# Expert pairs taken in another order, two of them before the routing is known, in a one-core network kernel

## The reference, cut to what matters

```python
def compress_blocks(x, pos_emb, w1, w2):          # once for keys, once for values, in each layer
    ...
    blk = blk.transpose(0, 1, 3, 2, 4).reshape(b_, n_cmp, NSA_GROUPS, CMP_LEN * NSA_DH)
    return jax.nn.silu(blk @ w1) @ w2             # w1: 32*64 x 64

def moe_ffn(h, w_router, w1, w3, w2):
    logits = (h @ w_router).astype(jnp.float32)
    top_val, top_idx = lax.top_k(logits, TOP_K)
    top_w = jax.nn.softmax(top_val, -1)
    combine = jnp.sum(jax.nn.one_hot(top_idx, N_EXPERTS, dtype=jnp.float32) * top_w[..., None], -2)
    out = jnp.zeros_like(h)
    for e in range(N_EXPERTS):
        out = out + combine[..., e:e + 1].astype(h.dtype) * swiglu(h, w1[e], w3[e], w2[e])
    return out
```

## Time and profile before

| | us |
|---|---|
| median of 3 runs | 2480.22 (2477.98 to 2480.71) |
| profiled execution, its own time | 2479.75 |
| its span, first to last instruction | 2477.9 |
| SP issues the first expert weight | 1577.17 |
| PE begins the first turn | 1590.66 |
| last instruction group on PE begins | 2467.38 |

### The profile page before, as it was taken

How to read it: one execution, slowest core, us unless ns; L and a number is a source line. 1 busy time by engine, 2 the same in 40 slices (tenths; PEclk the granted TensorE clock), 3 DMA queues, 4 the chain that set the end, 5 groups by cost and what they waited for, 6 DMA issues and landing times.

```text
span 2477.9 us, 35293 instructions
## 1 busy us (share of the span) xinstructions
PE 2348.5 (95%) x15259; PEld 1374.3 (55%) x15259; DVE 732.8 (30%) x1691; ACT 456.7 (18%) x905; POOL 48.4 (2%) x67
## 2 busy tenths in 40 slices
PE   7899999999999899999999999899999989999988
PEld 5655667856685447777677644544444334444433
DVE  2483475244454415242144442200001000000001
ACT  1222235523222411000132142200000000000000
POOL 3400000000000000000000000000000000000000
PEclk9999999999999999999999999899999999999999
DMA  8953564332222238675322120599999999999997
GB/s 265 205 204 145 184 236 167 129 130 91 81 95 78 83 125 307 232 275 200 136 70 104 70 102 34 210 409 409 401 384 398 403 407 403 402 401 409 408 404 272
DMA packets 210443, 586.51 MB, mean 237 GB/s; under 512 B 14672, under 2 KB 16800, under 8 KB 210288
## 3 DMA queue, kind: packets, MB, share of 16 engines
q1 hardware_dynamic: 206512, 576.93, 62.0%
q0 software_dynamic: 3376, 5.94, 1.3%
q10 hardware_dynamic: 400, 1.37, 0.2%
HBM read 583.16 MB, written 1.06 MB: 236 GB/s over the span
## 4 chain that ended last, share of the span: by engine, by line
PE 83%; DMA 6%; DVE 5%; ACT 3%; issue 1%; DVEq 1%; ACTq 0%; SPq 0%
PE PSB L2745 15%; PE PSA L387 10%; PE PSA L372 10%; PE PSB L2650 8%; PE PSA L2779 7%; PE PSB L2754 5%; DMA RING<-in_w_moe 4%; PE PSA L2630 4%; PE PSA L746 3%; PE PSA L2015 2%; PE PSA L2793 2%; PE PSA L1885 2%; PE PSB L2609 1%; PE PSB L1989 1%; PE PSB L1519 1%
## 5 line engine op out<-in xcount | busy, mean ns | idle before, releaser
L2745 PE MATMUL PSB<-RING,Y 128*64 128x512 f32 x1792 | 404.4, 603 | 29.8 <-DMA RING<-in_w_moe 13.2
L372 PE MATMUL PSA<-RING,HT 128*128 128x512 f32 (+1 forms) x704 | 300.8, 580 | 5.6 <-ACT Y L1490 2.9
L387 PE MATMUL PSA<-HT,RING 128*128 128x256 f32 x1216 | 279.6, 390 | 12.0 <-ACT PROJ L400 5.6
L2745 PEld LDWEIGHTS PSB<-RING,Y 128*64 128x64 f32 x1792 | 135.8, 139 | 270.2 <-issue 267.4
L387 PEld LDWEIGHTS PSA<-HT,RING 128*128 128x128 f32 x1216 | 236.0, 196 | 49.7 <-issue 15.9
L372 PEld LDWEIGHTS PSA<-RING,HT 128*128 128x128 f32 x704 | 131.2, 191 | 146.8 <-issue 142.7
L2779 PE MATMUL PSA<-RING,ROW 128*64 128x512 f32 x896 | 198.6, 595 | 5.8 <-issue 4.5
L2650 PE MATMUL PSB<-HT,RING 128*128 128x256 f32 x896 | 197.9, 379 | 1.6 <-issue 1.6
L2650 PEld LDWEIGHTS PSB<-HT,RING 128*128 128x128 f32 x896 | 170.2, 190 | 36.0 <-issue 14.2
L2901 DVE TENSOR_TENSOR PROJ<-PROJ,PSB 128x512 f32<-128x512 f32 x28 | 18.2, 685 | 552.9 <-PE PSB L2745 552.9
L2754 PEld LDWEIGHTS PSB<-RING,Y 128*32 128x32 f32 (+1 forms) x3136 | 107.4, 114 | 51.8 <-issue 41.5
(11 more groups left out here) (469 smaller groups left out, 2213.8 us busy)
## 6 DMA issues: line engine op xcount, KB each, us to landing
RING<-in_w_moe SPq DMA_DIRECT2D x166, 2048.0 KB, 18.8
RING<-in_w_ada SPq DMA_DIRECT2D x24, 2048.0 KB, 10.2
RING<-in_w_dense SPq DMA_DIRECT2D x21, 2048.0 KB, 12.8
RING<-in_w_in SPq DMA_DIRECT2D x20, 2048.0 KB, 7.7
RING<-in_w_in_c SPq DMA_DIRECT2D x15, 2048.0 KB, 7.7
RING<-in_w_in_ab SPq DMA_DIRECT2D x10, 2048.0 KB, 17.4
RING<-in_w_out SPq DMA_DIRECT2D x4, 2048.0 KB, 7.6
RING<-in_w_out_ab SPq DMA_DIRECT2D x3, 2048.0 KB, 7.7
```

What stands on the lines that cost most here:

```text
L372: mm = pe.matmul(PSA[:, lane[k], 512 * t:512 * t + cols], HT[:, c, P * t:P * t + P], W[:, c, 0:cols], start=(c == 0), stop=(c == KC - 1))
L387: mm = pe.matmul(PSA[:, lane[k], S * j:S * j + S], W[:, c, P * j:P * j + P], HT[:, c, :], start=(c == 0), stop=(c == KC - 1))
L2745: mm = pe.matmul(WIDE_BANKS[i][WIDE * which:WIDE * which + WIDE, :], HTG[:, c, WIDE * which:WIDE * which + WIDE], W[which][:, c - per * kh ...
```

## The change

- Experts 0 and 1 are the pair of turn 0, whatever their counts, with up to 96 and 64 places (`CAP_A`, `CAP_B`). Their 42 loads are issued from fixed addresses; the first seven wait for the slots alone (`last_in`, `scratch_free`) and not for `ranked`.
- The other six are sorted (`C_KEY` puts 0 and 1 last) and taken as 2nd with 5th, 1st with 6th, 3rd with 4th. The extra part is 32 places in turns 0 and 1 (`SOME`), 64 in turn 2 (`MOST`) and is left out in the last turn (`NONE`). The places cover the counts given above: 67 of 96 and 58 of 64 for experts 0 and 1; 84 of 96 with 47 of 64; 102 of 128 with 40 of 64; 60 and 54 of 64 each. So there are four turns as before.
- Turns 0 and 1 are written out, the loop body runs once, then the last turn.
- The selection of turn 0 is made before the sort, gathers of turn 0 and 1 have 160 columns, those of turn 2 and 3 have 192. The final scatter adds one product per piece in place of two. In the last turn `down` of a stage's first group stands ahead of `turned_wide`.
- Compression: keys stand on rows 0 to 63 and values on rows 64 to 127, so 4 transposes in place of 8, products of keys and values alternate, and the weights come in two loads of 0.5 MB in place of one of 1 MB. Every later item of the ring moves one slot on.

```diff
+        LOOPED = 2
         WIDE = P // 2
-        EXTRA = (P // 2, P // 4)
+        Extra = namedtuple("Extra", "width parts groups")
+        NONE = Extra(0, 0, ())
+        MOST = Extra(P // 2, 2, tuple((0, j, 64 * j, 64, P) for j in range(2)))
+        SOME = Extra(P // 4, 4, tuple((0, j, 32 * j, 32, P) for j in range(4)))
+        CAP_A, CAP_B, CAP_LAST = (96, 96, 128, 128), (64, 64, 64, 64), 64
...
-            L["cmp"] = item(I["w_cmp1_2"][l].rearrange("k (l d) e -> d (k l) e", d=NSA_D))
+            L["cmp"] = [item(I["w_cmp1_2"][l, kind].rearrange("(l d) e -> d l e", d=NSA_D)) for kind in range(2)]
+            part_of[L["cmp"][1]] = NSA_D
...
+            for i in range(CMP_LEN):
+                for kind in range(2):
+                    r = NSA_D * kind
+                    mm = pe.matmul(PSA[0:NSA_D, lane[k], 512 * kind:512 * kind + 33], W[kind][:, i, :],
+                                   XT[r:r + NSA_D, i:i + 2 * S + 1:CMP_STRIDE], start=(i == 0), stop=(i == CMP_LEN - 1))
...
+            dve_select(dve, 0)
+            dve.drain().then_inc(sem("select"), 1)
             dve.max(rank_sorted, rank_key)
...
+        def extra(turn, end=False):
+            if end:
+                return NONE
+            return SOME if isinstance(turn, int) and turn < LOOPED else MOST
...
+            def release(mm, which, last, wide):
+
+                if last and (which == 1 or not wide or not ex.groups):
+                    mm.then_inc(sem("item_used"), 1)
...
             for hf in range(2):
                 pe.wait_ge(sem(f"last_columns{hf}"), 32)
-                down_wide(GROUPS - 1, (512 * hf,), False)
-                down_extra(GROUPS - 1, (512 * hf,)).then_inc(sem("last_rows"), 1)
+                down_wide(GROUPS - 1, (512 * hf,), False).then_inc(sem("last_rows"), 1)
...
+                if isinstance(turn, int) and turn == 0 and j < SLOTS:
+                    if slot < MIX_SLOTS:
+                        sp.wait_ge(sem("item_used"), released(last_in[slot]))
+                    else:
+                        sp.wait_ge(sem("scratch_free"), DEPTH)
...
+            for j in range(PER_TURN):
+                load_item(0, j, [slice(0, 1), slice(1, 2)])
             sp.wait_ge(sem("ranked"), 1)
```

More of the change, by code:

```diff
@@ L1 @@
+from collections import namedtuple
 from contextlib import ExitStack
@@ L276, in network @@
         assert PER_TURN % SLOTS == 0
+        next_mixer = (items[-1][1] + 1) % MIX_SLOTS
+        TURN_SLOT = [(next_mixer + j) % MIX_SLOTS for j in range(MIX_SLOTS)] + list(range(MIX_SLOTS, SLOTS))
+        last_in = {slot: max(n for n, i in enumerate(items) if i[1] == slot) for slot in range(MIX_SLOTS)}
         row_list = []
@@ L2741, in first @@
                 per = KC // n
+                order = (0, 1) if ex.groups else (1, 0)
                 for i in range(n):
                     for c in range(per * kh, per * kh + per):
-                        for which in range(2):
+                        last = i == n - 1 and c == per * kh + per - 1
+                        for which in order:
                             mm = pe.matmul(WIDE_BANKS[i][WIDE * which:WIDE * which + WIDE, :],
@@ L2766, in turned_extra @@
             def turned_extra(u):
-                pe.wait_ge(sem("moe_hidden1"), staged(turn, u))
+                if not ex.groups:
+                    return
+                pe.wait_ge(sem("moe_hidden1"), extra_staged(turn, u))
                 for i in range(len(STAGES[u])):
@@ L2886, in act_moe_turn @@
                 if u == len(STAGES) - 1 and not end:
-                    take_misc(SCATTERS + 1)
-                    take_misc(SCATTERS + 2)
+                    for n in range(gathers(turn) - 1):
+                        take_misc(SCATTERS + 1 + n)
                 take_extra(u)
             if not end:
-                take_misc(SCATTERS + 3)
+                take_misc(SCATTERS + gathers(turn))
         def dve_moe_turn(dve, turn, end=False):
-            pw = 512 * extra(turn) // P
-            begun = not isinstance(turn, int)
+            ex = extra(turn, end)
+            pw = 512 // ex.parts if ex.groups else 0
+            begun = not (isinstance(turn, int) and turn == 0)
             def hidden_wide(u):
-                dve.wait_ge(sem("item_used"), used(turn, (1, "up", (u, len(STAGES[u]) - 1))))
+                wide_done(dve, turn, ex, "up", u)
                 for i, g in enumerate(STAGES[u]):
@@ new lines, in _ @@
+            sp.wait_ge(sem("ranked"), 1)
+            sp.reg_mov(ring[N_EXP - 1], 0)
+            sp.reg_mov(ring[3], 1)
+            for at, rank in zip((0, 1, 2, 4, 5, 6), (1, 0, 2, 4, 5, 3)):
+                sp.reg_mov(ring[at], sp.value_load(rank_i[0:1, rank:rank + 1].bitcast(I32), min_val=0, max_val=N_EXP - 1))
+            load_turn(1, range(PER_TURN))
+            next_pair()
+            last = turn_count(sp)
+            with sp.Fori(0, last) as turn:
+                load_turn(turn, range(PER_TURN))
+                next_pair()
@@ L3085, in _ @@
+            load_turn(last, range(PER_TURN - 2))
+            e = [sp.snap(ring[r], min_val=0, max_val=N_EXP - 1) for r in (0, N_EXP // 2)]
             for hf in range(2):
```

401 lines of the change are left out of this document (225 added, 176 removed).

## The result

| | before | after |
|---|---|---|
| median | 2479.1 (2477.95 to 2480.71) | 2442.43 (2441.22 to 2444.19) |
| ratio, with its 95% interval | | 0.9859 (0.9846 to 0.9872) |
| profiled execution, own time | 2479.75 | 2444.19 |
| its span | 2477.9 | 2442.4 |
| SP issues the first expert weight | 1577.17 | 1515.28 |

The change makes the kernel 36.7 us faster by the medians of four runs each and 35.5 us by the two spans. The profiled execution of after is the slowest of its four, 1.8 us above the median. The forecast was 2437, a gain of 43; the measured time is 5.4 us above it and inside the range. The miss has two signs: PE starts the experts earlier than forecast, and more than that lead is lost before the end.

What follows compares the result with a forecast made beforehand. The experts' DMA stream was taken as the bound: last data 2428.5 plus 10.4 after it gives 2438.9, less 4 for compression 2434.9, 43 under the span; from the median 2480.2 that gives 2437 us, range 2426 to 2454.

Steps and rivals of the forecast that it cites:

- What bounds the kernel: Experts: the DMA stream of 168 loads, 5.13 us each at 409 GB/s, 861 us in all, decides the end.
- The early stream: Start of the experts: seven loads need only their slots; 161 remain from 1594.2, and the earlier start is worth 21 us.
- The compression: Attention's compression in two layers: products on both row halves at once save 4 us, ends 8 and -2.
- The turns: PE's load by expert turn: 199 us for turn 0, about 216 for turn 1, 239.5 for turn 2.
- just not starved: End of turn 0: its last pair lands at 1773.8, before PE ends the turn at 1784.2.
- Turn 2 and the last data: Large extra part: PE ends at 2240.5 with a full ring; 36 loads from 2242.5 put the last data at 2428.5.
- The tail: After the last data: half a wide group 3.5 us, scatter 3.5, last addition and store 3.4; 10.4 in sum.
- now PE is ahead: Last turn: PE needs 167 us without data waits, has 20 us of cover, and is no longer behind by one pair.
- the rival of the cold PE: Last turn at half clock: about 2580 us, 4% together with more rounds; mild form, slow block starts, 2441 to 2444.
- the loop's entry or exit: Rival: PE gap on leaving the loop, +10 us, 2447; with one at entry, up to 2455; 16% with a late start.
- PE as the bound: Rival for the whole experts' part: the time follows PE's turns, 2402 us; chance 1%.
- no gain in the stream: Rival: early loads slow the routing or PE, leaving only the gain after the last data and 4 us: 2464; 4%.

Runs made afterwards that it cites:

- late_loads: The changed kernel, with SP waiting for the sorted expert numbers before the first load of experts, as before the change: 2464.22 us.
- small_extra: The changed kernel with turn 2's extra part held to 32 places in place of 64, leaving out 6 of 102 choices: 2430.89 us.
- late_small: The changed kernel with two edits: first expert loads wait for the routing, and turn 2 has 32 extra places in place of 64: 2454.45 us.
- last_extra: The changed kernel with the extra part of 32 places kept in the last turn: 2452.78 us.
- halves_in_turn: The changed kernel with the compression's products reordered, all 32 of the keys first, then all 32 of the values: 2447.99 us.

## Why the prediction was right, and by how much it was not

**What bounds the kernel: right.** (The rates of the earlier trace rows are 384 to 409 in the slices before the last, where the prediction wrote 381 to 411; nothing hangs on it.) The end is a stream of 5.13 us a load with a tail behind it. Products of 39 us in the last turn cost 9 to 10, and 7 loads that start early give 21.

**The early stream: right in kind and size.** The forecast gave it 21 us, late_loads 21.8 by the medians and 20.1 by the spans. PE's start: forecast 5.5 us earlier than before without the compression; measured 15.4 - 10.2 = 5.2.

**The compression: the term that was mis-sized.** Forecast 4 us with ends 8 and -2; measured 12 us (8 to 17) in the kernel that has nothing else, of which the traces show 6.8 us in the two compressions themselves (3.0 in layer 0, 3.8 in layer 1). The prediction read 55 ns a product off a merged row; from first start to last it is 58. The price of a full block was right all the same: 0.8 us forecast, 0.84 measured (1.81 to 0.97). What failed is the size of the step that took 3.2 of some 7.2 us back as waits. Waits did come back. The first block of each layer holds a pause, 0.73 us before and 1.50 after in layer 0, 0.92 and 1.55 in layer 1, and those two blocks save next to nothing; the wait for DVE of 1.33 us ahead of the second block in the earlier trace rows is 1.18 in after, and its counterpart in layer 1 grew from 1.69 to 2.56. The transposes gave 0.4 us in layer 0, as forecast. What made up for the waits isn't shown in full; TensorE's clock differs between the traces there. And 3.2 us of the lead at the end of attention (1.6 ahead of the compression, 1.6 a slow stretch of before) are the luck of the two executions. The Trainium skill, TensorEngine Tiling (Array Packing), Row Tiling, proposes two tiles of 64 rows for a contraction of 64, and the prediction named 7 us for both halves at once; the blocks of this case come near to that (0.97 us for 1.81), the kernel does not, since two blocks in eight gain nothing.

**The turns: right, each a little short.** Forecast against trace: turn 0 199 and 203.1, turn 1 216 and 219.5, turn 2 239.5 and 240.9. With the 4 us of the compression taken off, PE began the first turn 6.0 us ahead of forecast (1575.23 against 1581.2) and the stream resumed 5.9 ahead (1584.3 against 1590.2), yet turn 2 began 0.8 behind (1997.8 against 1997.0). PE's lead is worth nothing, since both turns end starved; the forecast said "just not starved" of turn 0, where PE waits three times, 1.2 to 1.9 us, between 1712 and 1738. The stream's lead went in two places. The 18th pair of turn 1 is the 71st load after the resumption, 71 x 5.13 = 364.2 us, and it came after 371.5 (1584.3 to 1955.8): 7.3 us where the forecast had 3. Only some 2.7 of these are lost rate (406 GB/s on average from 1584 to 1960), with the two dips of the 2 KB rows among them; the rest lies between the bytes moved and the start on PE, a step that the forecast put at nothing. And from that pair to the turn's end PE took 42.0 us, where the forecast let it end 9 us behind the last pair, 3 x 10.26 + 9 = 39.8: three pairs with gathers between them take longer than their transfers.

**Turn 2 and the last data: right in kind, 2.3 us short.** PE ends turn 2 at 2238.7, 2.2 us behind the forecast less 4. The forecast had the ring full there and the last data 187.9 us later; counted at the full rate they came after 190.2, at about 2428.9. That the full ring costs about what it holds back is seen in small_extra.

**The tail: 10.4 forecast, 13.5 measured.** Two things failed. The forecast took the end of the stream at the full rate, 2455.1 in before, for the last byte, which moved at 2459.1. In after the rate falls from 393 to 94 GB/s over the last 2.5 us, and the last byte moves at 2430.1, 1.2 us behind 2428.9. From the last byte the tail is 12.3 us, and 11.0 (0.6 above the sum) in the six other kernels without the extra part in the last turn. And the step "now PE is ahead" failed in the trace of after: `down` of group 5 starts with its data at 2419.9 and takes 8.78 us cold, and both halves of the last group follow it, the first of which should have been done by the time of the last data. That is the other 1.3 us. So the rival of the cold PE came true in its mild form: blocks that start slow about one in two, no hold on the stream, and 1.3 us at the end, less than the 3.5 to 7 it was given. The Trainium skill, TensorE: Matmul & The Clock Gate, on oscillation in real kernels, tells of a kernel that starts cold after each wait; the trace of after agrees for its waits of 2.2 us and more (8.8 us a block) and shows that those of 0.4 to 1.8 are followed by warm ones (7.09). It is no rule of this case: late_small has a block of 7.09 us behind a wait of 3.0. What the section counts as loss is here almost all hidden behind the transfers.

**The other rivals.** No gap appeared at the loop's entry or exit. In the kernel before, whose loop did return, PE idled some 9 us at 2031 to 2041, but its DMA ran at 409 and 408 GB/s in 2020 to 2060. PE was behind after it, and the ring filled: 402, 397 and 387 GB/s in 2060 to 2120 lack 2.0 us. That is the most that the gap can have cost, and no run tests it. PE as the bound (2402) is refuted by last_extra, and no gain in the stream (2464) by late_loads, which measures 2464.2, what that rival would look like.

**The sum of the parts.** Compression alone -12, early stream -20 to -22, extra part of the last turn -10; against it the hole of turn 2, +11.5, where the kernel before already lost 5.5 us behind its large turn 0 (five slices of 375 to 400 GB/s in 1800 to 1900) and 2.0 behind the loop, so +4. Together -38 to -40, and -36.7 is measured. The compression's term alone is uncertain by 4 us, so the sum agrees but does not test the parts.

## What to carry to other kernels

Where a queue of transfers sets the end, count the stage in transfers left and the time at which the stream resumes, and ignore when the compute engine starts: seven loads brought forward gave 21 us although PE began only 5 us earlier. A single stage that needs more compute than its transfers take makes a hole in the stream which a starved stage before or after it can't give back, and moving that stage did not help. Behind the last transfer every product counts in full, and so does the clock at which the engine enters it; work ahead of it costs little as long as waits are left. And before a difference of a few microseconds is put down to an edit, compare the stretches that the edit does not touch: here two traces of the same code differ by 1.7 to 2.6 us over eight products.

## What the runs showed of the hardware

- Two float32 products of 64 rows by 33 columns, on separate halves of the rows and in separate banks, start 31 ns apart on average; on one half 58 ns apart, with the same 232 ns for each. From first start to last in a block of 32 that is 0.97 against 1.81 us (after, before; with the halves in turn it is 1.8 again).
- In the last turn the granted clock fell for about one block in two. In after a block of 32 products took 8.8 us after waits of 2.2 to 3.8 us and 7.09 after waits of 0.4 to 1.8; late_small has one of 7.09 after 3.0. Filler of 1.98 us in the gap took nearly all of this away.
- Eight products of 128x512 behind the same wait of 1.46 us took 3.70 us in most traces, and 4.91 (before), 5.40 (late_small) or 6.29 us (halves_in_turn) in others; the granted clock fell to 0.50 for at least 2 us in these three.
- One core took 407 to 410 GB/s for hundreds of microseconds, with or without TensorE busy all through. In the slices of 20 us with the loads of 2 KB rows, in the last stage of the turns, it was 383 to 404.
- While PE idled for 9 us at the loop's return in before, DMA stayed at 408 and 409 GB/s.
